# A fused two-block transformer kernel: where scores, scaling and the biased pass of a late attention map stand, and when the first differential head's operands are copied

## The chip, the cores and the metric

The kernel runs on one core of a Trainium2 chip. The time is device microseconds of one execution, from the chip. Every execution computes both blocks for one sequence of 512 tokens with model width 1024. The engines are named as the profile does: PE (TensorE, matmuls and transposes), DVE (VectorE), ACT (ScalarE), POOL (GpSimd) and SP (SyncE, which here only issues DMAs).

## The reference

Two blocks follow each other. The first has two attentions, a merge and a feed-forward net; the second, which the change touches, projects the normed input to three kinds of heads, attends, multiplies by a gate and projects out:

```
proj = h @ w_in
cq, ckv, kr, dq, dk, dv, mq, z = split(proj)
# 8 latent heads ("mla"), causal, 96 wide
p = softmax(q @ k.T * 96**-0.5 + causal);  o = p @ v
# 4 differential heads ("diff"), causal, two maps each, 32 wide
a = softmax(q1 @ k1.T * s + causal) - lam * softmax(q2 @ k2.T * s + causal)
o = rms_norm(a @ v, subln_g) * (1 - lam_init)
# 4 memory heads ("mem"), 256 memory tokens, 64 wide
p = softmax(q @ k_mem.T / 8);  o = p @ v_mem
y = concat(mla, diff, mem) * silu(z);  x = x + y @ w_out
```

## The kernel before

All matrices are float32. Each is held as a rounded high part and a low part (BHI and BLO, HHI and HLO, XR for tiles of 128 x 512), and a product takes three matmuls. Weights come as 512 KB units through SP into RAW (two buffers), are rounded by ACT into WHI (L721), and the rest is taken by POOL into WLO (L642). SP issues the load of a unit when the low half of the unit before it has been made (`split_lo`), two units ahead of PE. All order is written out by hand: every engine runs its own program and waits on semaphores.

The last units before the stage that matters are z4, z3, z6, z5 (gate columns) and ukv. Then `attention("late")` runs over `LATE`, 20 maps in the order mla0, mla1, diff0 (two maps, 2 and 3), mla2, mla3, diff1 (6, 7), mla4, diff2 (9, 10), mla5, diff3 (12, 13), mla6, mem0 to mem3 (15 to 18), mla7. For each map:

- scores on PE (`scores`, L1920) write three PSUM banks, in groups; a group waits until the biased pass of the map before has read its bank.
- the biased pass on DVE (`biased`, L1314) subtracts in the causal mask, takes the row maximum and writes the probabilities' buffer. There are three such buffers, used in turn.
- ACT takes the exponential and its row sums (L879).
- the scaling (`normed`, L1327 and L1354; for the second map of a differential head L1352, which subtracts) multiplies by one over the sum; POOL does the widest block of a latent map (L659), half of a memory map (L705) and all of the first map of a differential head (L699).
- PE transposes (L1977), ACT copies the transposes to SBUF (L854), and PE multiplies them with the values (L2000).
- DVE multiplies a finished head by its gate (L1430), ACT rounds it (L923), DVE takes the low part (L1237). For a pair of differential heads ACT copies (L917) and squares (L920), PE sums (L2048), DVE inverts, ACT takes the root (L841), PE spreads it (L2032), and DVE applies it (L1378, L1381).

In step i PE and ACT run them in the order `scores(i+2), transposes(i), values(i-1)` and `copies(i-1), exponential(i+1), rounding(i-2)`; DVE runs `biased(i+1), normed(i)`, then the gates and low parts of heads finished by then. The first map of a differential head finds its queries and keys stacked four times over the 128 rows, in the tiles of `STACK`. SP makes the stacks with 16 copies of 64 KB for each head (`stack_heads`), and then the pairs for the memory heads (`pair_heads`), all after the load of the second output unit. HLO (lo(24) to lo(31)) holds the low part of the stage's input until z5 has been computed.

Of the kernel before, what the change touches and what calls it, by code (L numbers as in the profile page):

```python
# [109 lines left out]
def build(nc, t, out):  # L110
    from contextlib import ExitStack
    ctx = ExitStack()
    with ctx:
# [178 lines left out]
        ab = []  # L292
        heads = [(0, r, g) for r in range(4) for g in range(2)] + [(1, r, g) for r in range(4) for g in range(2)]
        for y, (blk, r, g) in enumerate(heads):
# [5 lines left out]
            else:  # L300
                for b, tile in ((1, 9), (2, 10)):
# [8 lines left out]
        LQ, LK, LV, PT_L = 0, (34, 35, 17, 18, 32, 33, 19, 16), (29, 30, 15, 14), (0, 1280)  # L310
        STACK = [[lo(24), lo(25), lo(26), lo(27)], [lo(28), lo(29), lo(30), lo(31)],
                 [lo(10), lo(11), lo(23), hi(31)], [lo(14), lo(15), hi(17), lo(17)]]
        dm = []
# [216 lines left out]
        def _(sp):  # L530
# [47 lines left out]
            stream_pairs((UNIT["down2"] + 1) // 2, UNIT["tail"] // 2, -4)  # L578

            def stack_heads():  # L580

                sp.wait_ge(h_lo, 4)
                sp.wait_ge(unit_used, UNIT["wout2"] - 1)
                for h in range(4):
                    if h == 3:
                        sp.wait_ge(unit_used, UNIT["wout2"])
                        sp.wait_ge(ATT["late"]["scores"], mla[2]["g1"])
                    for m in range(2):
                        f = 64 * (h % 2) + 32 * m
                        rows = slice(f, f + 32)  # L590
                        for at in range(4):
                            to = slice(32 * at, 32 * at + 32)
                            sp.dma_start(STACK[h][2 * m][to, :].bitcast(F), part(at % 2, DQ + h // 2)[rows, :].bitcast(F)).then_inc(stacked[h], 16)
                            sp.dma_start(STACK[h][2 * m + 1][to, :].bitcast(F), part(at // 2, DK + h // 2)[rows, :].bitcast(F)).then_inc(stacked[h], 16)

            def pair_heads():

                sp.wait_ge(h_lo, 8)
                sp.wait_ge(ATT["late"]["scores"], dm[3]["g1"])
                for h in range(4):  # L600
                    rows = slice(64 * (h % 2), 64 * (h % 2) + 64)
                    for w in range(2):
                        to = slice(64 * w, 64 * w + 64)
                        sp.dma_start(lo(24 + h)[to, :].bitcast(F), part(w, MQ + h // 2)[rows, :].bitcast(F)).then_inc(paired[h], 16)
                        for half in (slice(0, 64), slice(64, 128)):
                            sp.dma_start(lo(28 + h)[half, 256 * w:256 * w + 256].bitcast(F),
                                         part(w, MK)[rows, 256 * (h // 2):256 * (h // 2) + 256].bitcast(F)).then_inc(paired[h], 16)

            for c in range(UNIT["tail"] // 2 * 2, NPOS):
# [4 lines left out]
                sp.wait_ge(split_lo, c - 1)  # L614
                sp.dma_start(RAW[:, c % 2, :], w[at]).then_inc(raw_loaded[c % 2], 16)
                if c == UNIT["wout2"] + 1:
                    stack_heads()
# [555 lines left out]
        def _(dve):  # L1173
# [183 lines left out]
            def attention(name):  # L1357
                maps, pts = GROUP[name]
                A = ATT[name]
                for i in range(-1, len(maps) + (2 if name == "ab" else 3)):  # L1360

                    steps = [(biased, i + 1), (normed, i)]
                    for f, j in steps:
# [436 lines left out]
        def _(pe):  # L1800
# [210 lines left out]
            def attention(name):  # L2011
                maps, pts = GROUP[name]
                A = ATT[name]
                for i in range(-2, len(maps) + 2):
                    if name == "late" and i == 0:
# [6 lines left out]
                    if name == "ab" and i + 2 == 8:  # L2022
                        pe.wait_ge(cmp_lo, 1)
                    if 0 <= i + 2 < len(maps):
                        scores(A, maps[i + 2])
# [25 lines left out]
                    if 0 <= i - 1 < len(maps) and maps[i - 1].get("mode") != "hold":  # L2051
                        values(name, A, maps[i - 1], pts)
                    if name == "ab":
                        for u in TAIL.get(i, []):
# [325 lines left out]
```

## Time and profile before

| what | value |
|---|---|
| median of 3 runs | 1101.36 us (1099.15 to 1103.62) |
| the profiled execution | 1103.44 us, span 1101.4 us |
| PE busy | 1050.4 us, 95% of the span |
| ACT, DVE, POOL busy | 551.2, 623.1, 436.9 us |
| mean granted clock of PE | 0.986 |

The span is what the profile covers, from the first to the last instruction; the execution's own time holds some 2 us around it. A busy PE may still run at half its clock, so busy time and the granted clock are read together.

### The profile page before, as it was taken

How to read it: one execution, taken by the hardware profiler on the slowest of the kernel's cores; microseconds unless marked ns; L12 is line 12 of the kernel's file. 1: busy time of each engine (PE TensorE's matmuls, PEld its weight loads, DVE VectorE, ACT ScalarE, POOL GpSimd, SP SyncE). 2: the span in 40 equal slices, each digit the busy share in tenths (PEclk: the TensorE clock that was granted, in tenths of full speed). 3: DMA queues.
4: the chain of work that ended last, by engine and by line, in shares of the span. 5: the costliest groups of instructions: out<-in, count | busy, mean ns of one | idle time of the engine just before them, and what ended most of it. 6: DMA issues, size and time to landing. Idle time of an engine off the chain costs nothing.

```text
span 1101.4 us, 15071 instructions
## 1 busy us (share of the span) xinstructions
PE 1050.4 (95%) x5086; PEld 871.5 (79%) x5086; DVE 623.1 (57%) x1414; ACT 551.2 (50%) x1143; POOL 436.9 (40%) x227
## 2 busy tenths in 40 slices
PE   6999999899999999999999999999999979899798
PEld 3779888799888788888888888778887868666577
DVE  5547376988744466454545455442235979486732
ACT  6343465777634244444444444443244273888821
POOL 2356322233324444444444444414444244344322
PEclk9899999999999999999999999999999999898999
DMA  7564221111013422332322223243252222343213
GB/s 263 169 166 157 64 89 60 56 40 39 30 58 125 133 96 86 98 104 92 107 94 96 95 95 133 96 141 108 96 191 91 73 77 96 105 106 96 71 55 114
DMA packets 38811, 111.87 MB, mean 102 GB/s; under 512 B 5235, under 2 KB 8563, under 8 KB 38067
## 3 DMA queue, kind: packets, MB, share of 16 engines
q1 hardware_dynamic: 28572, 87.60, 24.5%
q10 hardware_dynamic: 8584, 18.89, 5.3%
q0 software_dynamic: 1600, 4.66, 1.1%
q8 instruction: 32, 0.52, 0.2%
q14 instruction: 23, 0.19, 0.1%
HBM read 100.25 MB, written 7.96 MB: 98 GB/s over the span
## 4 chain that ended last, share of the span: by engine, by line
PE 35%; issue 35%; POOL 13%; DVE 8%; ACT 4%; DMA 3%; SPq 1%; POOLq 0%; ACTq 0%; DVEq 0%
POOL WLO L642 11%; PE PS L1803 8%; PE PS L1805 8%; PE PS L1804 8%; PE PS L1977 2%; PE PS L2000 2%; DMA RAW<-wstream 2%; PE PS L1891 1%; PE PS L1936 1%; PE PS L1937 1%; DVE PB L1314 1%; PE PS L2139 1%; DMA X<-xT 1%; ACT WHI L721 1%; ACT PB L879 1%
## 5 line engine op out<-in xcount | busy, mean ns | idle before, releaser
L642 POOL TENSOR_TENSOR WLO<-RAW,WHI 128x1024 fp32r<-128x1024 f32 x147 | 355.7, 2420 | 530.7 <-ACT WHI L721 530.5
L721 ACT ACTIVATE WHI<-RAW 128x1024 fp32r<-128x1024 f32 x154 | 162.8, 1058 | 293.6 <-PE PS L1805 270.9
L1803 PE MATMUL PS<-HHI,WHI 128*128 128x512 f32 x648 | 256.6, 396 | 11.0 <-DVE HLO L1215 9.4
L1805 PE MATMUL PS<-HHI,WLO 128*128 128x512 f32 x648 | 253.7, 392 | 0.0
L1804 PE MATMUL PS<-HLO,WHI 128*128 128x512 f32 x648 | 253.6, 391 | 0.0
L1803 PEld LDWEIGHTS PS<-HHI,WHI 128*128 128x128 f32 x648 | 122.7, 189 | 39.4 <-issue 11.3
L1803 PE MATMUL PS<-BHI,WHI 128*128 128x512 f32 x368 | 145.2, 395 | 3.2 <-POOL WLO L642 1.8
L1805 PE MATMUL PS<-BHI,WLO 128*128 128x512 f32 x368 | 143.4, 390 | 0.0
L1804 PE MATMUL PS<-BLO,WHI 128*128 128x512 f32 x368 | 143.3, 389 | 0.0
L1805 PEld LDWEIGHTS PS<-HHI,WLO 128*128 128x128 f32 x648 | 122.5, 189 | 25.9
L1804 PEld LDWEIGHTS PS<-HLO,WHI 128*128 128x128 f32 x648 | 122.7, 189 | 25.6 <-issue 0.8
L1197 DVE TENSOR_TENSOR PS<-PS,PB 128x512 f32<-128x512 f32 x63 | 43.9, 697 | 86.9 <-PE PS L1805 85.3
L1237 DVE TENSOR_TENSOR BLO<-PS,BHI 128x256 fp32r<-128x256 f32 (+4 forms) x140 | 64.8, 509 | 38.9 <-ACT BHI L913 27.4
L1803 PEld LDWEIGHTS PS<-BHI,WHI 128*128 128x128 f32 x368 | 69.1, 188 | 20.5 <-POOL WLO L642 2.4
L879 ACT ACTIVATE PB<-PB,ST 128x256 f32<-128x256 f32 (+4 forms) x164 | 79.5, 501 | 4.8 <-DVE ST L1314 4.5
L1805 PEld LDWEIGHTS PS<-BHI,WLO 128*128 128x128 f32 x368 | 69.1, 188 | 14.7
L1804 PEld LDWEIGHTS PS<-BLO,WHI 128*128 128x128 f32 x368 | 69.1, 188 | 13.8
L1526 DVE SCALAR_TENSOR_TENSOR FX<-PS,CL,FX 128x511 f32<-128x511 f32 (+1 forms) x88 | 61.7, 743 | 12.0 <-ACT FX L973 11.8
L1803 PE MATMUL PS<-WHI,HHI 128*128 128x512 f32 (+2 forms) x128 | 48.7, 380 | 2.7 <-ACT PB L999 2.0
L1805 PE MATMUL PS<-WHI,HLO 128*128 128x512 f32 (+2 forms) x128 | 48.1, 376 | 0.0
L1804 PE MATMUL PS<-WLO,HHI 128*128 128x512 f32 (+2 forms) x128 | 47.8, 374 | 0.0
L854 ACT ACTIVATE BHI<-PS 128x256 fp32r<-128x256 f32 (+2 forms) x96 | 33.2, 415 | 26.7 <-PE PS L1972 16.1
(322 smaller groups left out, 1656.0 us busy)
## 6 DMA issues: line engine op xcount, KB each, us to landing
RAW<-wstream SPq DMA_DIRECT2D x154, 512.0 KB, 3.2
X<-xT ACTq DMA_DIRECT2D x4, 512.0 KB, 9.5
BF<-wstream POOLq DMA_DIRECT2D x2, 1024.0 KB, 7.0
BG<-wstream POOLq DMA_DIRECT2D x2, 1024.0 KB, 6.9
bias_b<-bias_rows ACTq DMA_DIRECT2D x2, 1024.0 KB
FX<-bias_b ACTq DMA_DIRECT2D x8, 256.0 KB, 2.7
X<-xT ACTq DMA_DIRECT2D x8, 256.0 KB, 3.7
x_keep<-X ACTq DMA_DIRECT2D x2, 1024.0 KB, 6.2
```

The costliest lines, as they stand in the source:

```text
L642: pool.tensor_tensor(WLO[:, s, :], RAW[:, s, :], WHI[:, s, :].bitcast(F), ALU.subtract).then_inc(split_lo, 1)
L721: act.activation(WHI[:, c % 2, :], RAW[:, c % 2, :], ACT.Copy).then_inc(split_hi, 1)
L854: ins = act.activation(to, src, ACT.Copy)
L879: ins = act.activation(dst, dst, ACT.Exp, bias=stat(m, NMAX)[:, q:q + 1], scale=-1.0, accum_out=stat(m, SUM)[:, q:q + 1])
L1197: dve.tensor_tensor(PS[:, bank, :], PS[:, bank, :], RSTD, ALU.mult).then_inc(scaled, 1)
L1237: return dve.tensor_tensor(dst_lo, src, dst_hi.bitcast(F), ALU.subtract)
L1526: dve.scalar_tensor_tensor(out=y, in0=PS[:, 2 * e + s, 0:SEQ - sh], scalar=cv[:, tap:tap + 1], in1=y, op0=ALU.mult, op1=ALU.add).then_inc( ...
L1803: pe.matmul(dst, a[0], b[0], start=first, stop=False, **kw)
L1804: pe.matmul(dst, a[0], b[1], start=False, stop=False, **kw)
L1805: return pe.matmul(dst, a[1], b[0], start=False, stop=last, **kw)
L1977: ins = pe.transpose(PS[:, 3 + b, o + j * P:o + (j + 1) * P], pr[:, p0:p0 + P], IDN[:, :])
L2000: ins = pe.matmul(PS[:, m["bank"], q0:q1], m["v"](kb), turned_block(m, pt, kb, 0), start=m["first"] and kb == 0, stop=m["last"] and kb == ...
```

## The change

The first differential head gets other tiles for its stack, free earlier, and its 16 copies are issued eight and eight behind the loads of units z4 and z3. The other heads' tiles move round, and the memory heads' keys are issued behind the scores of map 10. In the late stage PE's scores are written three maps ahead at the end of a step, and DVE scales map i ahead of the biased pass of map i+2.

```
-        STACK = [[lo(24), lo(25), lo(26), lo(27)], [lo(28), lo(29), lo(30), lo(31)],
-                 [lo(10), lo(11), lo(23), hi(31)], [lo(14), lo(15), hi(17), lo(17)]]
+        STACK = [[lo(10), lo(11), lo(23), lo(15)], [lo(24), lo(25), lo(26), lo(27)],
+                 [lo(28), lo(29), lo(30), lo(31)], [lo(14), hi(31), hi(17), lo(17)]]
...
+            def stack_part(h, m):
+
+                f = 64 * (h % 2) + 32 * m
+                rows = slice(f, f + 32)
+                for at in range(4):
+                    to = slice(32 * at, 32 * at + 32)
+                    sp.dma_start(STACK[h][2 * m][to, :].bitcast(F), part(at % 2, DQ + h // 2)[rows, :].bitcast(F)).then_inc(stacked[h], 16)
+                    sp.dma_start(STACK[h][2 * m + 1][to, :].bitcast(F), part(at // 2, DK + h // 2)[rows, :].bitcast(F)).then_inc(stacked[h], 16)
+
             def stack_heads():
 
-                sp.wait_ge(h_lo, 4)
                 sp.wait_ge(unit_used, UNIT["wout2"] - 1)
-                for h in range(4):
+                for h in range(1, 4):
...
                     for m in range(2):
-                        f = 64 * (h % 2) + 32 * m
...
+                        stack_part(h, m)
...
+                sp.wait_ge(ATT["late"]["scores"], dm[5]["g1"])
+                for h in range(4):
...
                 sp.dma_start(RAW[:, c % 2, :], w[at]).then_inc(raw_loaded[c % 2], 16)
+                if c in (tail("z4"), tail("z3")):
+                    sp.wait_ge(h_lo, 4)
+                    sp.wait_ge(unit_used, tail("u5") + 1)
+                    stack_part(0, (tail("z4"), tail("z3")).index(c))
...
-                    steps = [(biased, i + 1), (normed, i)]
+                    if name == "ab":
+                        steps = [(biased, i + 1), (normed, i)]
+                    else:
+                        steps = [(biased, 0), (biased, 1)] if i < 0 else [(normed, i), (biased, i + 2)]
...
-                for i in range(-2, len(maps) + 2):
+                for i in range(-2 if name == "ab" else -3, len(maps) + 2):
...
-                    if 0 <= i + 2 < len(maps):
+                    if name == "ab" and i + 2 < len(maps):
                         scores(A, maps[i + 2])
...
                         values(name, A, maps[i - 1], pts)
+                    if name == "late" and i + 3 < len(maps):
+                        scores(A, maps[i + 3])
```

On SP the kernel before issues all copies of head 0 behind the last 28 weight loads of this part (BHI to HLO are the first of them):

```order
L615 DMA RAW<-wstream 128x1024 [waits split_lo] x28
L593 DMA HLO<-BHI 32x512 [waits unit_used,head_lo]
L594 DMA HLO<-BHI 32x512
L593 DMA HLO<-BLO 32x512
L594 DMA HLO<-BHI 32x512
```

With the change they stand behind the 22nd and the 23rd load, eight and eight (the middle of each eight is left out here):

```order
L621 DMA RAW<-wstream 128x1024 [waits split_lo] x22
L586 DMA BLO<-BHI 32x512 [waits unit_used,head_lo]
L587 DMA BLO<-BHI 32x512
...
L621 DMA RAW<-wstream 128x1024 [waits split_lo]
L586 DMA BLO<-BHI 32x512 [waits unit_used,head_lo]
L587 DMA BLO<-BHI 32x512
...
L621 DMA RAW<-wstream 128x1024 [waits split_lo] x5
L586 DMA HLO<-BHI 32x512 [waits unit_used]
```

Five loads now follow, and then the copies of head 1, the first into HLO.

On DVE, around the scaling of map 3 (L1352 before, the second map of the first differential head), the kernel before has the low part of one head (L1237) and the gate of the next (L1430) between that scaling and the biased pass of map 5 (ISA, L1314):

```order
L1352 SCALAR_TENSOR_TENSOR PB<-PB,ST,X 128x512
L1237 TENSOR_TENSOR BLO<-PS,BHI 64x512 [waits late_y_hi]
L1430 TENSOR_TENSOR PS<-PS,FX 64x512 [waits late_pv]
L1314 ISA X,ST<-PS,TRI 128x256 [waits late_scores,late_turned,late_normed]
L1314 ISA ST 128x1
L1314 ISA X,ST<-PS,TRI 128x128 [waits late_scores]
```

With the change the whole biased pass stands ahead of both:

```order
L1362 SCALAR_TENSOR_TENSOR PB<-PB,ST,X 128x512
L1324 ISA X,ST<-PS,TRI 128x256 [waits late_scores,late_turned,late_normed]
...
L1324 ISA X,ST<-PS,TRI 128x512 [waits late_scores]
L1324 ISA ST 128x1
L1247 TENSOR_TENSOR BLO<-PS,BHI 64x512 [waits late_y_hi]
L1443 TENSOR_TENSOR PS<-PS,FX 64x512 [waits late_pv]
L1337 RECIPROCAL ST<-ST 128x4 [waits late_exped]
```

The two single instructions moved behind the four blocks of the pass, and the next scaling follows them as before.

On PE the order of the matmuls does not change. At the scores of map 2 the kernel before waits for the last projections (`head_lo`, `vm_hi`) as well as for the stack:

```order
L1947 MATMUL PS<-HLO 128x256 [waits stacked0,late_biased,head_lo,vm_hi]
L1947 MATMUL PS<-HLO 128x128 [waits late_biased]
L1947 MATMUL PS<-HLO 128x384
L1947 MATMUL PS<-HLO 128x512 [waits late_biased]
L1977 MATMUL PS<-IDN,PB 128x128 [waits late_normed]
```

With the change that wait stands at the transposes of map 0 behind them:

```order
L1960 MATMUL PS<-BLO 128x256 [waits late_biased,stacked0]
L1960 MATMUL PS<-BLO 128x128 [waits late_biased]
L1960 MATMUL PS<-BLO 128x384
L1960 MATMUL PS<-BLO 128x512 [waits late_biased]
L1990 MATMUL PS<-IDN,PB 128x128 [waits late_normed,head_lo,vm_hi]
```

What moved there is a wait and the tiles that the scores read.

## Rows read from the trace of the kernel before

**Rows 1.** The page: busy time, share of the span and instructions of each engine.
```profile
PE 1050.4 (95%) x5086; PEld 871.5 (79%) x5086; DVE 623.1 (57%) x1414; ACT 551.2 (50%) x1143; POOL 436.9 (40%) x227
```

**Rows 2.** Busy time by stretch: whole late stage, then one microsecond of its start.
```profile
core 0: us, PE busy (x) PEld busy (x) DVE busy (x) ACT busy (x) POOL busy (x), PEclk, DMA share, GB/s
951.40:1054.40 103.00, 86.43 (x433) 63.48 (x434) 70.33 (x252) 83.42 (x263) 42.44 (x34) 0.92 0.33 89
...
954.00:955.00 1.00, 0.00 (x0) 0.00 (x0) 0.00 (x0) 1.00 (x5) 1.00 (x1) 0.50 0.36 88
```

**Rows 3.** Timeline of PE, start of the late stage: start, duration, instruction, idle before.
```profile
956.55 1.51 PE L1947 MATMUL PS<-HLO 128*128 128x256 f32 x4 [5.20 <-DMA HLO<-BLO]
957.86 2.34 PE L1977 MATMUL PS<-IDN,PB 128*128 128x128 f32 x10
...
961.96 1.67 PE L2000 MATMUL PS<-HF 128*128 128x512 f32 x4
...
966.03 1.67 PE L2000 MATMUL PS<-HF 128*128 128x512 f32 x4
```

**Rows 4.** SP's queue, one ACT row of a unit, and the page's DMA list.
```profile
907.74 0.33 SPq L615 DMA_DIRECT2D RAW<-wstream  x1
...
913.97 0.33 SPq L615 DMA_DIRECT2D RAW<-wstream  x1
...
920.26 0.33 SPq L615 DMA_DIRECT2D RAW<-wstream  x1
...
944.75 0.62 SPq L593 DMA_DIRECT2D HLO<-BHI  x1
...
954.28 0.59 SPq L594 DMA_DIRECT2D HLO<-BLO  x1
...
919.98 1.07 ACT L721 ACTIVATE WHI<-RAW 128x1024 fp32r<-128x1024 f32 x1
...
RAW<-wstream SPq DMA_DIRECT2D x154, 512.0 KB, 3.2
```

**Rows 5.** Timeline of ACT: exponential of map 2, rounding of map 1, copies of map 4.
```profile
960.78 0.52 ACT L879 ACTIVATE X<-X,ST 128x256 f32<-128x256 f32 x1
...
971.10 0.59 ACT L923 ACTIVATE BHI<-PS 64x512 fp32r<-64x512 f32 x1 [1.86 <-DVE PS L1430]
...
975.24 1.49 ACT L854 ACTIVATE HF<-PS 128x256 f32<-128x256 f32 x5
```

**Rows 6.** Timeline of DVE: n0, b2, n1, gate of map 0, n3, n5.
```profile
955.07 0.18 DVE L1327 RECIPROCAL ST<-ST 128x4 f32<-128x4 f32 x1 [2.97 <-ACT PB L879]
...
957.14 0.43 DVE L1314 CUSTOM_DVE_ANT_0 X<-PS,TRI 128x256 f32<-128x256 f32 x1 [0.98 <-PE PS L1947]
...
958.98 0.17 DVE L1327 RECIPROCAL ST<-ST 128x4 f32<-128x4 f32 x1
...
964.32 0.69 DVE L1430 TENSOR_TENSOR PS<-PS,FX 64x512 f32<-64x512 f32 x1 [1.05 <-PE PS L2000]
...
967.74 1.94 DVE L1352 SCALAR_TENSOR_TENSOR PB<-PB,ST,X 128x256 f32<-128x256 f32 x4 [0.52 <-POOL X L699]
...
976.18 0.17 DVE L1327 RECIPROCAL ST<-ST 128x4 f32<-128x4 f32 x1
```

**Rows 7.** Timeline of POOL: widest block of map 0, all of map 2.
```profile
955.73 1.78 POOL L659 TENSOR_SCALAR PB<-PB,ST 128x512 f32<-128x512 f32 x1 [0.50 <-DVE PB L1354]
...
963.36 4.27 POOL L699 TENSOR_SCALAR X<-X,ST 128x128 f32<-128x128 f32 x4 [1.95 <-DVE ST L1325]
```

**Rows 8.** Waits of the late stage: who for whom, total us, times, longest.
```profile
ACT BHI L923 <- DVE PS L1430: 15.3, 7, 3.5
```

**Rows 9.** Timelines of DVE, ACT and PE near the end of the late stage.
```profile
1037.45 0.75 DVE L1378 SCALAR_TENSOR_TENSOR PB<-PB,CL,PS 128x512 f32<-128x512 f32 x1 [2.10 <-PE PS L2032]
...
1038.96 0.63 ACT L907 ACTIVATE BHI<-PB 128x512 fp32r<-128x512 f32 x1 [0.58 <-DVE PB L1381]
...
1045.91 3.41 PE L2000 MATMUL PS<-HF,BF 128*128 128x512 f32 x4
```

More of the change, by code:

```diff
@@ L588, in stack_heads @@
                     for m in range(2):
-                        f = 64 * (h % 2) + 32 * m
[L590 to L594, printed above, removed]
+                        stack_part(h, m)
             def pair_heads():
@@ L602, in pair_heads @@
                     for w in range(2):
-                        to = slice(64 * w, 64 * w + 64)
-                        sp.dma_start(lo(24 + h)[to, :].bitcast(F), part(w, MQ + h // 2)[rows, :].bitcast(F)).then_inc(paired[h], 16)
+                        sp.dma_start(lo(24 + h)[64 * w:64 * w + 64, :].bitcast(F), part(w, MQ + h // 2)[rows, :].bitcast(F)).then_inc(paired[h], 16)
+                sp.wait_ge(ATT["late"]["scores"], dm[5]["g1"])
+                for h in range(4):
+                    rows = slice(64 * (h % 2), 64 * (h % 2) + 64)
+                    for w in range(2):
                         for half in (slice(0, 64), slice(64, 128)):
```

## The prediction

> **What bounds the kernel now.** I read the page first: TensorE (PE) is busy for 95% of the span [rows 1], so the time is PE's, plus whatever idle time sits between its instructions. The change touches only the last attention stage ("late", 20 maps, 951 to 1054 us) and the weight loads ahead of it, so the next view is the stretch table. In those 103.0 us PE is busy 86.4, ACT 83.4, DVE 70.3 and POOL 42.4, at a mean granted clock of 0.92 [rows 2]: no engine fills the stage, it is a chain that passes between them. The timeline of PE then gives the one large hole. The scores of map 2, the first differential one, start at 956.55, after 5.20 us in which PE had nothing (so those of map 1 ended at 951.35), and a copy into HLO released them [rows 3]. The SP queue says why: it starts these copies at 944.75, issues one every 0.63 us, starts the sixteenth at 954.28, and the data is there 2.0 us later [rows 4]. The remaining views ask what else is late at that place, since a stall is worth only the distance to the next late thing.
>
> In what follows s, b, e, n, t, v are scores (PE), biased pass (DVE), exponential (ACT), scaling (DVE), transposes (PE) and values (PE) of a map. y_f is the multiplication of a finished head by its gate (DVE L1430), y_hi its copy by ACT (L923), and R(i) is what DVE does at the end of step i, y_f among it.
>
> **Part 1, copies of head 0 issued earlier: their own cost.** Sixteen copies leave the block at 944.75 and stand eight each behind two loads that started at 907.74 and 913.97; the next load started at 920.26 [rows 4]. Eight copies take 8 x 0.63 = 5.1 us. 907.74 + 0.6 + 5.1 = 913.4, ahead of 913.97 by 0.5; 913.97 + 5.7 = 919.7, ahead of 920.26 by 0.6. So no weight load is issued later: cost 0. Should this cover be missed, ACT converts the second of these units only at 919.98, 6.0 us after its load started, and a load in this kernel lands in 3.2 us as the page's list of issues has it [rows 4], so 2.8 us more are hidden. The copies have landed by 922, 29 us before s2 needs them. Heads 1 and 2 then start at 944.75 instead of ten and twenty us later: cost 0. The keys of the memory heads wait for s10, some 16 x 0.63 = 10 us of issue, and are wanted five maps later: cost 0.
>
> By the Trainium skill, "DMA: Bandwidth & Descriptors", section "Issuing engines are not separate DMA queues", all these copies share the same 16 engines with the weight loads. If so, a load would wait for its company of eight 64 KB copies, as much data as itself, so an estimate from the load's own 3.2 us is at most 3.2 more, the size of the slack above and no more; no run shows it yet.
>
> **Part 2, what the stall is really worth.** With s2 free it runs from 951.4 to about 952.7, its last block waiting for b1. Then t0 needs n0, and DVE starts n0 at 955.07, after 2.97 us of waiting for ACT's e0 [rows 6]; t0's widest block needs POOL, 955.73 + 1.78 = 957.51 [rows 7]. So PE waits about 3 us again, and t0 ends near 958.4 instead of 957.86 + 2.34 = 960.2 [rows 3]. On DVE b2 follows n0 at 956.2 instead of 957.14, and n1 starts at 958.0 instead of 958.98 [rows 6]: gain 1.0. POOL's part of map 1 moves by as much, and v0 starts at 961.0 instead of 961.96 [rows 3]: 0.9. On ACT e0 and e1 are unmoved; the last copies of t0, two blocks in 0.66 us or so, end at 959.1, so e2 starts there instead of 960.78 [rows 5]: 1.7. POOL's hold pass follows, 961.6 instead of 963.36, four passes of 4.27 us in all [rows 7]. Of 5.20 us, 0.9 to 1.7 survive the first ten microseconds.
>
> **Part 3, DVE's order.** PE's order of matmuls is the same before and after (scores of i+3 at the end of a step stand where scores of i+2 stood at the start of the next); only its wait for the last projections moves behind s2. On DVE every R(i) moves behind b(i+2). A biased pass of a causal map takes 957.14 to 958.98, 1.84 us [rows 6]. The price is first seen at y_f of map 0: at 964.32 it lay in DVE time that waited for PE [rows 6]. Now b4 goes first, but s4 follows v0, and the two take 966.03 - 961.96 = 4.07 us [rows 3], to 965.1, so b4, whose last block can start only then, ends at 965.75, y_f at 966.4, and n3 starts its products at 966.8, though POOL is done at 965.9. It was 967.74 [rows 6]: 0.9 left instead of 1.8. Next n3 (1.9), b5 (1.8), y_lo and y_f of map 1 (1.4) end at 972.0, so y_hi of map 1 on ACT starts at 972.0 where it started at 971.10 [rows 5]: ACT is now 0.9 late. Behind it e5 would end at 976.15 instead of 975.24 [rows 5], and n5, which started at 976.18 [rows 6], starts at 976.2. The head start is gone: 0.
>
> From there the same trade repeats: y_hi waits for y_f on ACT, 15.3 us in seven places already [rows 8], and each such wait grows by up to 1.84. Walking on with the same durations I find ACT 1.6 late behind y_hi of map 4 and 1.9 behind map 5, but DVE, which has the longer queue there, asks for e8 2.7 us after it ends. That slack covers it: cost 0. Some 0.3 lost at n8 is won back where b12 no longer stands behind the wait for the sums of squares. The bounds of this term are 0 and, without the cover, 1.9 per place.
>
> **Part 4, the end.** Late in the stage DVE waits 2.10 us for PE's spread, does R(17) from 1037.45 [rows 9], and only then b19. Now b19 fills the wait (its scores stand on PE ahead of the very spread that DVE waits for) and 1.6 to 1.8 us leave the chain y_f, b19, n18, POOL, t18, v17 at 1045.91 [rows 9]. ACT, late by something between 0.9 and 1.84 as above (I take 1.2), had only 0.58 us to spare before its copy at 1038.96 [rows 9]; it gives back 0.6. Gain 1.0.
>
> **Sum.** 0 (copies) + 0 (stall, eaten by step 5) + 0 (middle) - 1.0 (end) = -1.0 us. The profiled execution took 1103.44 with a span of 1101.4 and some 2 us around it, so it would be 1102.4; the median of the runs shown is 1101.36, 2.1 below the profiled one, and the forecast on it is **1100.4 us**. A measurement of this kernel can tell about 0.5%, 5.5 us, from no change; its three runs alone spread over 4.5.
>
> **Rivals.**
> - *The head start survives.* If ACT's copies have more slack than I walked, 0.9 to 1.7 from the start and 1.6 from the end add up: 2.5 to 3.3, about 1098.4. For it: seven waits of ACT on y_f are short of work, not of time. Against it: n5 had no wait of its own. At most all of the 5.20 and 1.6 come: 1094.6.
> - *The reordering costs (the other side).* Place: y_hi on ACT and what is queued behind it, the copies of transposes and the next exponential. Price 1.9 per place where the exponential is wanted at once. It decides once ACT is more than 2.7 us late at e8. Two such places less 1.0: +2.8, 1104.2. To be over 5.5 us slower, four of the seven must cost their whole pass.
> - *The clock.* While PE stood idle before s2 the granted clock fell from full to 0.50, that is to 1.2 GHz [rows 2], and the ten transposes of t0 took 2.34 us [rows 3]; at twice the clock that is some 1.2. PE now waits 3 us in place of 5.2. If it stays at 2.4 GHz, up to 1.1 more is gained at t0: 1099.3. If the new pattern of waits catches v17 or v7 otherwise, whose four matmuls took 3.41 us [rows 9] and would take half of it at full clock, it moves by up to 1.7 either way. By the Trainium skill, "TensorE: Matmul & The Clock Gate", Part 1, the slow clock is the resting state and activity lifts it; the row agrees.
> - *The change does nothing visible on the path*: within 0.5 us, 1101.4.
> - *Copies push a weight load past its slack*: needs over 2.8 us of delay on top of 0.5; then +1 to +2, 1103.
>
> **How the numbers follow.** Forecast (-2 to +0.5, 1099.4 to 1101.9) 0.40; head start survives 0.20; reordering costs 0.18; clock alone 0.10; nothing 0.08; copies delay 0.04. For the range I leave out the far ends of rivals one and two and add the spread of the medians: 1096.5 to 1104.8. Faster by over 5.5 us needs the whole stall and the end together: 0.06. Slower by over 5.5 needs four full passes: 0.05. Same: 0.89.
>
> **What would show it.** Right: no PE wait on a copy before map 2, but a wait of about 3 us on DVE's scaling before t0; loads at 913.97 and 920.26 not later relative to their release; v0 about 0.9 earlier, n5 where it was; waits of ACT's y_hi on y_f grown from 15.3 to over 20 us; b19 ahead of the spread, POOL's pass of map 18 about 1 us earlier. Wrong: an early head start still visible at v3 (975.7 before), or exponentials late enough that DVE waits on ACT in the middle of the stage.

## The result

| | before | after |
|---|---|---|
| median, 15 runs each | 1103.51 us (1099.06 to 1106.31) | 1106.54 us (1102.71 to 1111.98) |
| ratio, 95% interval | | 1.0033 [1.0021, 1.0046] |
| profiled execution, span | 1101.4 us | 1104.6 us |
| mean granted clock | 0.986 | 0.983 |

By the ratio the change costs 3.6 us of 1103.5 (0.33%; the two medians stand 3.0 apart), inside the 0.5% called "same", but the interval excludes zero, and a gain of 1.0 had been forecast. The time of after lies above the forecast range.

What the change touches on PE lies in one stage, and from the start of PE's last values (map 19) to the end of the span 47.5 to 47.7 us pass in every trace, so the stage is read by itself. Two executions of one kernel can reach it microseconds apart. I therefore measure its length from a weight load, the next one after the load at 920.26 of [rows 4] (923.57 before, 923.46 after), to the start of the last group of values of map 19: **130.17 us before and 133.54 after, +3.4**. Where an experiment's trace groups that load with others, its time is taken from the last projection ahead of the stage, which stood 26.9 us behind it where both were read. The two ends, before and then after:

```profile
1053.74 0.82 PE L2000 MATMUL PS<-HF,BF 128*128 128x256 f32 x4
1057.00 0.82 PE L2013 MATMUL PS<-HF,BF 128*128 128x256 f32 x4
```

**The profile after.** The page's first part, and the stretch table for the late stage and for two single microseconds (columns as in [rows 2]):

```profile
PE 1053.8 (95%) x5086; PEld 872.7 (79%) x5086; DVE 624.2 (57%) x1414; ACT 550.7 (50%) x1143; POOL 437.0 (40%) x227
```

```profile
954.00:955.00 1.00, 0.00 (x0) 0.00 (x0) 0.00 (x1) 1.00 (x5) 1.00 (x1) 0.50 0.50 123
951.40:1054.40 103.00, 85.80 (x422) 62.82 (x422) 69.75 (x249) 81.33 (x259) 42.39 (x34) 0.88 0.29 79
975.00:976.00 1.00, 1.00 (x5) 0.78 (x4) 0.63 (x1) 1.00 (x4) 0.00 (x0) 0.50 0.33 80
```

PE's busy time grew by 3.4 us with the same 5086 matmuls, and the granted clock of that stretch fell from 0.92 to 0.88 (the stretch ends at 1054.40 in both traces, 2.6 us ahead of the last group of values after). That is the first hint: the same work took longer. The last row is a microsecond in which PE was busy throughout, at half its clock.

SP's queue, where the first copies of head 0 now stand (start, duration):

```profile
908.04 0.62 SPq L586 DMA_DIRECT2D BLO<-BHI  x1
...
912.51 0.59 SPq L587 DMA_DIRECT2D BLO<-BLO  x1
913.86 0.33 SPq L621 DMA_DIRECT2D RAW<-wstream  x1
...
918.65 0.60 SPq L587 DMA_DIRECT2D BLO<-BLO  x1
920.16 21.14 SPq L621 DMA_DIRECT2D RAW<-wstream  x5
```

Both loads start 0.1 us earlier than before, as does the whole trace here. The copies are hidden.

PE's timeline through the late stage (start, duration, idle before and releaser), against [rows 3] and [rows 9]:

```profile
955.71 1.56 PE L1990 MATMUL PS<-IDN,PB 128*128 128x128 f32 x6 [3.13 <-DVE PB L1364]
...
961.08 1.67 PE L2013 MATMUL PS<-HF 128*128 128x512 f32 x4
...
973.25 2.40 PE L1990 MATMUL PS<-IDN,PB 128*128 128x128 f32 x10 [2.02 <-DVE PB L1364]
975.44 3.33 PE L2013 MATMUL PS<-HF,BF 128*128 128x512 f32 x8
...
992.62 1.94 PE L1990 MATMUL PS<-IDN,X 128*128 128x128 f32 x10 [2.03 <-DVE X L1364]
994.40 4.02 PE L2013 MATMUL PS<-HF,BF 128*128 128x512 f32 x8
...
1008.50 2.08 PE L2045 MATMUL PS<-IDN,PB 128*128 128x128 f32 x8 [2.74 <-ACT PB L851]
...
1024.66 2.46 PE L1990 MATMUL PS<-IDN,X 128*128 128x128 f32 x10 [1.19 <-DVE X L1364]
1026.91 3.20 PE L2013 MATMUL PS<-HF,BF 128*128 128x512 f32 x8
...
1049.05 3.52 PE L2013 MATMUL PS<-HF,BF 128*128 128x512 f32 x4
```

The stall of 5.20 us on the copy is gone and 3.13 us on DVE stand in its place. v0 starts at 961.08 instead of 961.96. Then come waits that before had in smaller pieces, and behind them values that ran slow. The same three groups of values before (maps 3, 7 and 13):

```profile
975.67 2.32 PE L2000 MATMUL PS<-HF,BF 128*128 128x512 f32 x8
...
993.20 2.90 PE L2000 MATMUL PS<-HF,BF 128*128 128x512 f32 x8
...
1023.86 2.32 PE L2000 MATMUL PS<-HF,BF 128*128 128x512 f32 x8
```

Those of map 3 (eight matmuls) took 3.33 us instead of 2.32, those of map 7 4.02 instead of 2.90, those of map 13 3.20 instead of 2.32: 3.0 us in all. The wait of 2.74 us at the spread is new (before, PE had waited 0.87 and 0.30 us just ahead of it, for the biased pass of map 12): PE's spread of the first differential pair waits for ACT's root. DVE and ACT show why it is late:

```profile
1001.39 1.94 DVE L1362 SCALAR_TENSOR_TENSOR PB<-PB,ST 128x256 f32<-128x256 f32 x4
1003.37 0.42 DVE L1324 CUSTOM_DVE_ANT_0 PB<-PS,TRI 128x256 f32<-128x256 f32 x1
...
1005.13 0.69 DVE L1443 TENSOR_TENSOR PS<-PS,FX 64x512 f32<-64x512 f32 x1
1005.74 0.15 DVE L1447 TENSOR_SCALAR SS<-PS 128x8 f32<-128x8 f32 x1
```

```profile
1005.92 0.59 ACT L933 ACTIVATE BHI<-PS 64x512 fp32r<-64x512 f32 x1 [3.19 <-DVE PS L1443]
...
1007.82 0.63 ACT L851 ACTIVATE PB<-SS 128x512 f32<-128x512 f32 x1
```

Between the scaling of map 10 and the gate of map 8 stands the biased pass of map 12. The gate and the root in the kernel before:

```profile
1001.04 0.69 DVE L1430 TENSOR_TENSOR PS<-PS,FX 64x512 f32<-64x512 f32 x1
1003.73 0.63 ACT L841 ACTIVATE PB<-SS 128x512 f32<-128x512 f32 x1
```

Both came 4.1 us later with the change: on ACT the rounding that waits for y_f stands ahead of the root. Two views of waits, from 880 us on (the first line before, the two others after):

```profile
ACT BHI L923 <- DVE PS L1430: 17.1, 8, 3.5
ACT BHI L933 <- DVE PS L1443: 23.3, 11, 3.4
DVE ST L1337 <- ACT PB L889: 6.1, 4, 3.0
```

Over the shorter stretch of [rows 8], 951.4 to 1054.4, ACT's waits on y_f grew from 15.3 to 20.6 us.

Following the lag against before along PE: -0.9 us at v0, +0.8 at s7, +2.3 at s11, +3.0 at the spread, +3.9 at s17 (1029.86 against 1025.94) and, after the end's gain, +3.3 at v19 (1055.39 against 1052.14). Across the wait for the root, then, only 0.7 us are lost; from v0 to s17 it is 4.8, and 3.0 of these are the three slow groups of values.

### The profile page after: what moved, and what is told of

Its sections match the earlier page's. It is cut to its first block, busy times and chain, and to the rows that moved or that the text cites. A ratio compares the mean times of both kernels' runs of the same rounds, so it can differ in the third digit from the quotient of the medians.

```text
span 1104.6 us, 15071 instructions
## 1 busy us (share of the span) xinstructions
PE 1053.8 (95%) x5086; PEld 872.7 (79%) x5086; DVE 624.2 (57%) x1414; ACT 550.7 (50%) x1143; POOL 437.0 (40%) x227
## 4 chain that ended last, share of the span: by engine, by line
PE 36%; issue 35%; POOL 12%; DVE 8%; ACT 5%; DMA 3%; POOLq 0%; ACTq 0%; DVEq 0%
POOL WLO L652 11%; PE PS L1816 8%; PE PS L1818 8%; PE PS L1817 8%; PE PS L1990 3%; PE PS L2013 2%; DMA RAW<-wstream 2%; PE PS L1904 1%; PE PS L1949 1%; PE PS L1950 1%; ACT PB L889 1%; DVE PB L1324 1%; ACT WHI L731 1%; PE PS L2154 1%; DMA X<-xT 1%
## 5 line engine op out<-in xcount | busy, mean ns | idle before, releaser
L1816 PEld LDWEIGHTS PS<-BHI,WHI 128*128 128x128 f32 x368 | 69.1, 188 | 20.6 <-POOL WLO L652 2.5
L1817 PEld LDWEIGHTS PS<-BLO,WHI 128*128 128x128 f32 x368 | 69.1, 188 | 13.7
L1990 PE MATMUL PS<-IDN,PB 128*128 128x128 f32 x270 | 40.3, 288 | 12.1 <-DVE PB L1364 5.2
L1990 PEld LDWEIGHTS PS<-IDN,PB 128*128 128x128 f32 x270 | 32.0, 147 | 21.0 <-issue 8.7
```

The costliest lines, as they stand in the source:

```text
L1816: pe.matmul(dst, a[0], b[0], start=first, stop=False, **kw)
L1817: pe.matmul(dst, a[0], b[1], start=False, stop=False, **kw)
L1990: ins = pe.transpose(PS[:, 3 + b, o + j * P:o + (j + 1) * P], pr[:, p0:p0 + P], IDN[:, :])
```

## The experiments

Each was run about 12 times (e12 6 times) beside 29 to 35 runs of the kernel before on the same chip, whose medians were 1102.56 (e1 to e4), 1102.78 (e5 to e8), 1103.07 (e9 to e12) and 1103.12 us (e13 to e15). The ratio is against those runs, with its 95% interval, and not the quotient of the medians shown here. "Stage" is the length defined above, "slow work" PE's busy time lost to half clock: over slices of 1 us from 24 us after the load to the end of the stage, busy time times (1 - granted clock). "Idle" is PE's idle time in the same slices. These three are from one trace of each kernel.

| kernel | median, us | ratio | stage | slow work | idle |
|---|---|---|---|---|---|
| before | 1103.51 | 1 | 130.2 | 6.8 | 16.6 |
| after | 1106.54 | 1.0033 [1.0021, 1.0046] | 133.5 | 10.5 | 17.2 |
| e15 after again | 1106.01 | 1.0031 [1.0017, 1.0046] | 132.7 | 9.4 | 17.6 |
| e1 copies only | 1101.85 | 0.9990 [0.9975, 1.0006] | 130.2 | 8.1 | 15.0 |
| e2 order only | 1104.47 | 1.0008 [0.9991, 1.0025] | 132.1 | 8.2 | 18.8 |
| e3 after, PE kept busy | 1102.02 | 0.9996 [0.9979, 1.0013] | 131.2 | 4.7 | 14.3 |
| e4 gate first | 1099.65 | 0.9965 [0.9953, 0.9978] | 127.3 | 7.1 | 13.7 |
| e5 gate first, copies of before | 1101.16 | 0.9985 [0.9971, 0.9999] | 127.6 | 7.1 | 15.2 |
| e6 gate first, maps 0 to 5 | 1102.24 | 0.9998 [0.9982, 1.0014] | 130.8 | 10.0 | 14.9 |
| e7 gate first, map 8 on | 1100.42 | 0.9979 [0.9963, 0.9995] | 128.7 | 4.9 | 16.9 |
| e8 e4, PE kept busy | 1097.98 | 0.9955 [0.9937, 0.9973] | 126.4 | 5.6 | 13.3 |
| e9 gate first, map 8 alone | 1103.90 | 1.0008 [0.9989, 1.0027] | 130.3 | 6.5 | 16.5 |
| e10 gate first, map 11 on | 1103.23 | 0.9999 [0.9986, 1.0013] | 131.0 | 7.8 | 17.6 |
| e11 e2, PE kept busy | 1101.79 | 0.9999 [0.9984, 1.0014] | 131.7 | 5.6 | 14.9 |
| e12 e8 with more of it | 1096.08 | 0.9938 [0.9916, 0.9960] | 124.2 | 0.0 | 11.9 |
| e13 before, PE kept busy | 1101.32 | 0.9993 [0.9981, 1.0005] | 128.9 | 3.0 | 13.2 |
| e14 after, PE kept busier | 1101.35 | 0.9992 [0.9979, 1.0006] | 129.9 | 4.6 | 11.2 |

The stage of one trace and the ratio agree on the distance to before within 1.7 us for every kernel. The split into slow work and idle time is coarser. What is left of the 106.2 us before when both are taken off is 82.8, and for the other kernels without added matmuls it is 81.1 (e2) to 83.3 (e9), although their matmuls are the same; so differences of one or two microseconds in these columns say little. Nor is a microsecond of slow work a microsecond of the stage: e11 has 2.6 less of it than e2 and is 0.4 us shorter, e12 has 7.1 less than e4 and is 3.1 shorter.

The record has the mean granted clock of every execution too. Over the 126 of the kernel before beside the experiments its mean is 0.9856, over the 27 of the changed kernel (15, and 12 of e15) 0.9830. Among the 126, each 0.001 more of it goes with 0.68 us less time (correlation -0.70). At that rate, an estimate (it is an association within one kernel and not a price), the difference of 0.0026 stands for 1.8 us, about half of the loss. So the lower clock is no matter of one trace.

The letters of the theories start anew with e5, with e6 and with e9. In e1 to e4 A says that DVE's order and what follows from it costs and that the early copies do not, B that the order costs nothing and the copies or the moved tiles do, and C (e3, e4) that the loss is the half clock behind the longer waits.

**Two halves of the change.** e1 takes back DVE's order:

```
-                    if name == "ab":
-                        steps = [(biased, i + 1), (normed, i)]
-                    else:
-                        steps = [(biased, 0), (biased, 1)] if i < 0 else [(normed, i), (biased, i + 2)]
+                    steps = [(biased, i + 1), (normed, i)]
```

> The changed kernel with the DVE order of before: biased pass of map i+1, scaling of map i, then the gates. Tiles and early copies as changed. Theory A (the DVE order costs, the copies are free): the stall of 5.2 us before map 2 becomes one of about 3 us before the transposes of map 0, the head start of about 0.9 us is not lost again, and the time is 1 to 3 us under before, ratio 0.998. Theory B (the copies or the moved tiles cost): 3 us over before, ratio 1.003.

Measured 0.999, stage 130.2. That rules out B. In the trace the early copies remove the stall and are worth nothing at the end; the interval, [0.9975, 1.0006], leaves room for a gain.

e2 is the kernel before with the lines marked - above.

> The kernel before with only DVE's order changed: scaling of map i, biased pass of map i+2, then the gates. Copies as before. Theory A: the whole loss and no head start to set against it, 4 us over before, ratio 1.0035 to 1.0045. Theory B: no change, 1.000.

Measured 1.0008 with an interval of [0.9991, 1.0025]: less than A expected, and by the runs alone not to be told from no change. The stage is 1.9 us longer. Its trace has the same gathered waits as after:

```profile
975.44 2.49 PE L1980 MATMUL PS<-IDN,PB 128*128 128x128 f32 x10 [2.02 <-DVE PB L1354]
```

Both halves together (+3.4) cost more than their sum (+1.9). In the traces the slow work of e2 is 2.3 us less than that of after (idle time 1.6 more): v13 (2.32 us) and v17 (1.88) ran at full clock there, v10 (3.33 against 2.32) did not. How much of that belongs to the copies and how much to the execution is not shown: a second trace of the changed kernel (e15 below) has 9.4 instead of 10.5.

**The clock.** e3 is the changed kernel with matmuls of two constant tiles on PE, two ahead of the transposes of maps 4 and 8, one ahead of those of 14, written into the bank that the values overwrite next (the output is unchanged):

```
+                    if name == "late" and i in WARM:          # {4: 2, 8: 2, 14: 1}
+                        bank_free(name, A, maps[i - 1])
+                        for _ in range(WARM[i]):
+                            pe.matmul(PS[:, maps[i - 1]["bank"], :], IDN[:, :], TRI[:, :], start=True, stop=True, skip_group_check=True)
```

> The changed kernel with five idle-time matmuls on PE (constant operands, their result is overwritten): two each ahead of the transposes of maps 4 and 8, one ahead of those of map 14, where PE waits 2.02, 2.03 and 1.19 us in the changed kernel and its granted clock falls to 0.50 behind the wait. Each takes some 0.85 us. Theory C (the loss is the half clock that follows the longer waits): values of maps 3, 7 and 13 take 2.3 us instead of 3.3, 4.0 and 3.2, and 2.5 to 3.5 us are won, ratio 1.000 to before. Theory A (lateness of the gates alone): nothing is won, ratio 1.003, or more where a matmul is late.

Measured 0.9996, stage 131.2. Five added matmuls, put into waits, took 2.3 us off the stage, and v3, v7 and v13 ran in 2.32 us each, as C said. PE's rows, of a pair (each matmul is two rows) and of the values behind it:

```profile
973.60 1.98 PE L2056 MATMUL PS<-TRI,IDN 128*128 128x512 f32 x4
...
977.30 2.32 PE L2018 MATMUL PS<-HF,BF 128*128 128x512 f32 x8
```

**The gate's place.** e4 moves y_f alone, ahead of the biased pass:

```
-                        steps = [(biased, 0), (biased, 1)] if i < 0 else [(normed, i), (biased, i + 2)]
+                        steps = [(biased, 0), (biased, 1)] if i < 0 else [(normed, i), (gated, i - 2), (biased, i + 2)]
```

> The changed kernel with only the gate multiplication of a finished head moved back ahead of the biased pass (scaling of i, gate of i-2, biased pass of i+2, then the low parts and the sums). Theory A: the loss sits in the gate, for which ACT waits with the rounding, the copies and the next exponential: the waits of ACT on it fall from 23.3 us to about 15 and the ratio to before is 0.998 to 1.000. Theory C: PE's single long waits before maps 4 and 8 stay, and of the 3 us less than 1 comes back, ratio 1.002 to 1.003.

Measured 0.9965, better than expected and than both kernels. PE's waits of 2.0 us are short pieces again, the wait for the root is 0.49 us instead of 2.74, and ACT waits 13.3 us for y_f over the late stage (the second view, of waits) instead of 20.6:

```profile
968.24 1.18 PE L1993 MATMUL PS<-IDN,PB 128*128 128x128 f32 x6 [0.56 <-DVE PB L1364]
970.11 0.90 PE L1993 MATMUL PS<-IDN,PB 128*128 128x128 f32 x4 [0.69 <-POOL PB L669]
970.80 3.81 PE L2016 MATMUL PS<-HF,BF 128*128 128x512 f32 x8
...
987.04 1.64 PE L1993 MATMUL PS<-IDN,X 128*128 128x128 f32 x6 [0.57 <-DVE X L1364]
...
1000.98 1.98 PE L2048 MATMUL PS<-IDN,PB 128*128 128x128 f32 x8 [0.49 <-ACT PB L851]
```

```profile
ACT BHI L933 <- DVE PS L1376: 13.3, 7, 3.4
```

Yet v3 ran slow here too, behind waits of 0.56 and 0.69 us: shorter waits do not keep the clock by themselves. Most of what e4 gains over before is idle time (13.7 us against 16.6), not clock: its slow work is 7.1 against 6.8 us, and the mean granted clock of its 12 executions, 0.9870, is 0.0014 above before, 1.0 us of 3.9 by the estimate above.

e5 is e4 with the copies of before.

> The kernel before with the new order on DVE and the gate's multiplication ahead of the biased pass, but with the copies of before: the stall of 5.2 us before map 2 is there again. Theory A (the order costs only by the gate's place; the early copies are worth what they moved, 0.9 us at the first values): about 1 us above the version with gate first and early copies, so ratio 0.9975. Rival B (the copies give back most of their 5.2 us now that nothing eats the head start): 3 us or more above it, ratio 0.999 to 1.001. Rival C (gate first alone explains everything and copies do nothing): same as that version, 0.9965. In the trace: from the last weight load's issue (before 923.57) to the last values (1053.74), 130.2 us before, 133.5 with the change, 127.3 with gate first; A says 128.3, B 130.3, C 127.3.

Measured stage 127.6, between A (128.3) and C (127.3): in the trace the copies are worth 0.3 us even where nothing eats their head start. By the ratios, 0.9985 against 0.9965, they would be worth 2.2 us; the intervals overlap, and what the copies give here is not settled.

**Which gates.** e6 and e7 move y_f of some heads only, by adding `and m["n"] <= 6` (maps 0, 1, 4, 5) or `> 6` to the condition.

> The changed kernel with the gate's multiplication ahead of the biased pass for the first four latent heads alone (maps 0, 1, 4, 5); the others behind it as in the change. Theory A (the loss is made in the first half: exponentials late behind y_hi, small waits gathered, slow clock at v3 and v7, late root of the first differential pair): most comes back, last weight load to last values 129 us, ratio about 0.998. Rival B (the loss is made evenly, each place its own): half, about 130.5, ratio 1.000. Rival C (made late): 132 or more, ratio 1.002.

> The complement: gate first for maps 8, 11, 14 and the memory heads, behind the biased pass for maps 0, 1, 4, 5. Theory A: the first half's loss stays (+2.3 us at the scores of map 11, where the changed kernel had it), the rest of the growth is gone; last weight load to last values about 131, ratio 1.001. Rival B: about 130.5. Rival C: 129 or less, ratio 0.998.

I had the places wrong: it is the late gates (128.7, 0.9979) that bring most, the early ones half (130.8, 0.9998), though the two intervals overlap. Either alone takes 2.7 or 4.8 us off 133.5, both together 6.2, so they are not a sum of places. e9 and e10 split the late ones (`== 7`, which is map 8, and `> 7`).

> The changed kernel with one single multiplication moved: that of the fifth latent head (map 8) stands ahead of the biased pass, all others behind it as in the change. Theory D (the loss of the middle is one place: y_f of map 8 was 4.1 us late, y_hi of map 8 stands on ACT ahead of the root of the first differential pair, and the spread on PE then waits 2.7 us for that root): the wait goes to 0.5 us, last weight load to last values 133.5 - 2.3 - some clock = 130 to 131, ratio about 1.0000. Rival E (the loss is spread over all the late heads): only 1 us or less comes back, 132.5 or more, ratio 1.0025.

> The complement among the late heads: gate first for maps 11, 14 and the memory heads, behind the biased pass for maps 0, 1, 4, 5 and 8. Theory D: the wait for the root (2.7 us) stays, and 131 to 132.5 us from last weight load to last values, ratio 1.001 to 1.002. Rival E: 130.5 or less, ratio 1.000.

With the one multiplication of map 8 moved the wait for the root is gone; without it, it stays. The rows of e9 and e10, from the views of waits:

```profile
PE PS L2051 <- ACT PB L851: 0.5, 1, 0.5
```

```profile
PE PS L2051 <- ACT PB L851: 2.7, 1, 2.7
```

e9 came out as D said in the stage (130.3, 3.3 us less; ratio 1.0008). But e10, which keeps that wait, is also 2.5 us shorter: 131.0 is at D's edge, its ratio of 0.9999 is what E expected, and by the runs it is no worse than e9. D with one single place falls. What both have in common is the slow work, 4.0 and 2.7 us less than after, while the idle time hardly moved (-0.7, +0.4). Part of that is the execution and not the edit: v3 and v7 come ahead of anything that either edit moves, and they took 2.32 and 3.44 us in e9, 2.32 and 3.27 in e10, and 3.33 and 4.02 in after. The repeated trace of the changed kernel (e15) has 2.32 and 3.44 too. So 1.6 to 1.8 us of each gain in the trace are no gain of the gates; the ratios, 0.25% and 0.34% below after's, are the better witness that both edits help.

e11 is e2 with the added matmuls of e3.

> New order alone (copies of before), with extra matmuls on PE ahead of the transposes of maps 4, 8 and 14 in the waits of 2.0 us for DVE; their result is overwritten. With the early copies the same extra matmuls took 2.3 us off (133.5 to 131.2). Clock theory of the difference between the change and the order alone (133.5 against 132.05): with the clock held in both, both come to the same place, 131.2, less or more 0.4, ratio 1.000. Rival (the early copies cost something else): 130 or less here.

Stage 131.7, 0.5 us above e3 (expected within 0.4), ratio 0.9999 beside 0.9996: with PE kept busy in its waits, the order costs the same with and without the early copies, within what a trace tells. That fits an excess of the change over the order alone that was clock; with differences this near to the scatter of single traces it does not prove it.

**The clock raised in both kernels.** e8 adds one such matmul to e4 ahead of the transposes of maps 4 and 8; e12 one more ahead of those of 12 and three ahead of those of 0.

> Gate first, early copies, and one extra matmul (its result is overwritten, so the computation is unchanged) on PE ahead of the transposes of maps 4 and 8, where PE waits 0.56 and 0.57 us for DVE and v3 afterwards ran at half clock (3.81 us for 8 matmuls, 2.32 at full). Clock theory: v3 at full clock, the transposes of map 8 too, 1 to 2 us faster than without it: last weight load to last values 125.5 to 126.5, ratio about 0.9955. Rival (a single idle spell of 0.5 us is not what lowers the clock, or the gain is eaten by the next wait for DVE): no change, 127.3, ratio 0.9965; or slower by the 0.5 us that each extra matmul lasts.

> The fastest version so far (gate first, early copies, one extra matmul ahead of the transposes of maps 4 and 8) with one more ahead of those of map 12 (PE waits 1.05 us there and 0.98 behind it, then ran at half clock from 1016 to 1023 us) and three ahead of those of map 0, in the wait of 3.12 us. Clock theory: the transposes of maps 0 and 1 at full clock (1.55 and 1.12 and 2.01 us become 0.8, 0.6 and 1.3), v13 2.32 instead of 3.23 us: last weight load to last values 126.4 minus 1 to 2.5, ratio 0.994. Rival (DVE and ACT are next behind PE there, so that the time goes into waits): 126.4, ratio 0.9955.

e8 gained 0.9 us over e4 in the trace, e12 3.1, and both came out as the clock theory said. In the trace of e12 the granted clock is full through the whole stage, from before the first transposes on (its stage ends at 1044.06; the stretch is the one used above):

```profile
951.40:1054.40 103.00, 91.25 (x478) 67.04 (x478) 73.16 (x253) 81.05 (x255) 41.19 (x34) 1.00 0.27 75
```

e13 and e14 raise it in the kernel before (five added in the stall, one each ahead of the transposes of maps 8 and 12) and in after (e3 and three more ahead of map 0).

> The kernel before with extra matmuls on PE (their result is overwritten): five while it waits for the copies of map 2, one each ahead of the transposes of maps 8 and 12. Clock theory: the half-clock work at the start and at the values of map 7 goes, 6.8 us at half clock become about 3, and the late stage (last weight load to last values, 130.2 before) takes 127.5 to 129; ratio about 0.998. Rival (the order and its waits set the time): 130.2, ratio 1.000.

> The changed kernel with three extra matmuls ahead of the transposes of map 0 and two, two and one ahead of those of maps 4, 8 and 14. Clock theory: 129 to 130 us, within 1 us of the kernel before treated alike, ratio 0.998. Rival (the order costs by itself, through the late gates and the wait for the root): 1.5 us or more behind the kernel before treated alike, 130 to 131, ratio 1.000.

> The changed kernel as it is, once more, on the chip of the two others: ratio 1.003 and 133.5 us if its six spells at half clock belong to it in every execution; a ratio of 1.001 or less would say that its loss differs from chip to chip.

The two come to 1101.32 and 1101.35 us, ratios of 0.9993 and 0.9992: the distance of 3.6 us between the kernels has gone, give or take 2 us by the two intervals. Both ratios lie between the clock theory's 0.998 and the rival's 1.000. In the traces after is 1.0 us longer (129.9 against 128.9), where 3.4 us lay between the kernels as they stand. The clock is not equal in the two, though. Slow work is 3.0 us in e13 and 4.6 in e14, the mean granted clock over their executions 0.9907 and 0.9896, and behind the wait for the root, 2.85 us in e14, where nothing was added, v10 ran slow (e13 first, then e14):

```profile
1004.04 2.32 PE L2005 MATMUL PS<-HF,BF 128*128 128x512 f32 x8
1010.36 3.24 PE L2018 MATMUL PS<-HF,BF 128*128 128x512 f32 x8
```

e15, the change once more, is again 1.0031, and its trace says that the slow spells aren't bound to one wait: the same wait as at 973.25 in the first trace, and values at full clock behind it:

```profile
975.78 1.95 PE L1990 MATMUL PS<-IDN,PB 128*128 128x128 f32 x10 [2.02 <-DVE PB L1364]
977.57 2.32 PE L2013 MATMUL PS<-HF,BF 128*128 128x512 f32 x8
```

Its stage is 2.6 us longer than before's, its slow work 2.6 us more; in the first trace the two were 3.4 and 3.7.

## Why the prediction was wrong, by its own steps

**The base.** The forecast of 1100.4 stood on a median of three runs, 1101.36, and the median of fifteen is 1103.51. So 2.2 us of the 6.1 between the forecast and 1106.54 are the base. With the same margins around 1103.5 the range would have held the measured time; the sign of the change would still have been wrong.

**Part 1 held.** Copies cost nothing: loads at 913.86 and 920.16, and e1 is not slower. The two loads with eight copies behind them landed 3.5 us after their issue each (3.2 and 3.3 before), 0.2 to 0.3 us later, where the prediction had 3.2 us more as the most, and ACT converted the second of them at 919.88, as before.

**Part 2 held**: PE's next wait was forecast as "about 3 us" and was 3.13, v0 as 961.0 and was 961.08. In the trace of e1 the head start does not reach the end even with DVE's old order.

**Part 3 held for its first fifteen microseconds and is the step that failed after them.** n3 was to start at 966.8 (966.97), y_hi of map 1 at 972.0 (972.11), n5 at 976.2 (976.39). "That slack covers it: cost 0" was the error: the head start of 0.9 us at v0 was to be lost and no more, and the trace loses 4.8 us from v0 to s17. The walk asked for one thing only, whether DVE would wait for ACT's exponentials. It left out two consequences of the same late y_f:
- *The clock.* DVE's biased pass ahead of y_f gathers PE's short waits before the transposes into one of 2.0 us, and PE's work behind it may run at half clock. Term in the sum: 0. Measured: +3.7 us of slow work in one trace, +2.6 in the other, for a stage longer by 3.4 and 2.6; 3.0 us at v3, v7 and v13 of the first. With the clock raised (e13, e14) 2.4 of 3.4 us go in the traces and the medians are equal within 2 us. The mean clock of all executions accounts for about half of the loss by the estimate above. So it is shown that the clock carries a good part of the loss; its share, from half to nearly all, is not. The rival on the clock named t0, v7 and v17 and gave 1.7 us either way; v3 and v13, where it also struck, were not in it.
- *The root of the differential pair.* The prediction looked at this place for the biased pass of map 12 alone, which "no longer stands behind the wait for the sums of squares" (it did gain: it came 0.3 us later than before in place of 2.3), and not for what now stands behind that pass. The gate of map 8 went from 1001.04 to 1005.13 (2.3 of these 4.1 us were lag already, the rest is the pass of map 12), and on ACT the rounding queued on it stands ahead of the root: 2.74 us of wait on PE. e9 removes just that. The wait itself costs little, 0.7 us of lag in the trace after, and e14, which keeps it, is 1.0 us behind e13 in all; v10 at half clock behind it is 0.9 of that.

What the order costs by itself, at a clock that is equal in both kernels, is therefore not measured; e13 and e14 say that it is 1.0 us or less in the stage and nothing that the medians show. That the place of y_f is behind the whole loss, clock and waits together, is shown by e4: moved ahead of the biased pass, with all else as changed, it turns 1.0033 into 0.9965.

**Part 4 held**: DVE's wait for the spread shrank from 2.10 to 0.20 us, and the lag falls from +3.9 us at s17 to +3.1 at v17 (1049.05 against 1045.91), 0.8 given back where 1.0 was forecast.

Of the rivals, "the reordering costs" had the sign (1104.2, +2.8 on the three-run median), but its mechanism, late exponentials, is a small part: DVE's waits for those in the buffer PB grew from 3.2 to 6.1 us (2.98 at n0, as before, 0.46 at n13, 0.82 at n15 and 1.83 at n19), and waits of 0.77 us at n5 and at n9 are new beside them. The clock's rival had the mechanism without the size or the places. Of the listed signs, those for right came true (3 us wait, loads, ACT's wait over 20 us, b19 ahead of the spread) though the sum was wrong: none of them looked at PE's clock in the middle. One sign for wrong came too, in a small size: DVE waited for exponentials at n5, n9, n13 and n15, where it had not before.

Left open: why a given wait is followed by slow matmuls in one execution and not in the next, and how the loss divides between clock and order. What would shorten the stage at full clock with the gate first (e12: idle 11.9 us, 3.5 of it on the low parts before the values) wasn't tried.

## What to carry to other kernels

When an operation is moved behind a longer one on its engine, walk everything queued on it to the engine that sets the end, and ask there not only how long it waits but whether short waits become one long one: in this kernel PE often paid for them a second time, in matmuls at half clock. Split a trace's difference into idle time and busy time lost to the clock before looking for a wait, and take more than one trace of each kernel: here two traces of one kernel differ by 1.0 us at one group of values. A single small operation put first (the gate, 0.69 us) turned a loss of 0.33% into a gain of 0.35%, and a few matmuls on constants in PE's waits made it 0.6%.

## What the hardware showed unexpectedly

- The same kernel with the same wait of 2.02 us ran the eight matmuls behind it in 3.33 us in one execution and 2.32 in another. In e4, waits of 0.56 and 0.69 us were followed by 3.81 us. The Trainium skill, "TensorE: Matmul & The Clock Gate", Part 1, says of a kernel's start that the number of its slow matmuls varies from run to run. The two traces agree, in the middle of a kernel. A list of waits alone did not tell here which matmuls would be slow.
- Six matmuls on constants in PE's waits (e12; together 6.0 us of PE's timeline) cost no time: the granted clock of the stretch was 1.00 in its trace instead of 0.88 to 0.92, and the stage 3.1 us shorter than e4's. The traced execution had the highest mean clock of its six, 0.997; four others had 0.990 to 0.995, and one 0.942.
- SP's sixteen copies of 64 KB each between weight loads of 512 KB moved neither of the next loads (913.97 and 920.26 before, 913.86 and 920.16 after) and lengthened the landing of the loads ahead of them only from 3.2 and 3.3 to 3.5 us.
